# Second mixer: decayed keys and queries built by doubling blocks out of products of f, in place of logarithm, scan and exponentials

## The reference, cut to what matters

```
f = lbf + (1.0 - lbf) * jax.nn.sigmoid(f_logit)      # decay of every key channel and token, between 0 and 1
k = 1.0 - f
logf = jnp.log(f)
...
ac = jnp.cumsum(to_chunks(logf, A_KDIM), axis=3)
def step(S, inp):
    o_inter = jnp.einsum('bhtk,bhkv->bhtv', q_ * jnp.exp(a_), S)
    diff = a_[:, :, :, None, :] - a_[:, :, None, :, :]
    decay = jnp.exp(jnp.where(causal, diff, -jnp.inf))
    scores = jnp.einsum('bhtsk,bhsk->bhts', q_[:, :, :, None, :] * decay, k_)
    o = o_inter + jnp.einsum('bhts,bhsv->bhtv', scores, v_)
    S = jnp.exp(a_last)[..., None] * S + jnp.einsum('bhsk,bhsv->bhkv', k_ * jnp.exp(a_last - a_), v_)
```

## Time and profile before

| what | value |
|---|---|
| median of 3 runs | 2967.06 us (2964.86 to 2969.84) |
| the profiled execution | 2965.61 us, of which the span of its instructions 2963.5 us |
| PE busy | 2866.3 us (97%) |
| DVE busy | 2015.3 us (68%) |
| ACT busy | 1204.7 us (41%) |
| POOL busy | 1214.6 us (41%) |
| slots of `mixer2` in the trace | 1447 to 2037 us |

### The profile page before, as it was taken

How to read it: one execution, slowest core, us unless ns; L and a number is a source line. 1 busy time by engine, 2 the same in 40 slices (tenths; PEclk the granted TensorE clock), 3 DMA queues, 4 the chain that set the end, 5 groups by cost and what they waited for, 6 DMA issues and landing times. The chain is left out here.

```text
span 2963.5 us, 55833 instructions
## 1 busy us (share of the span) xinstructions
PE 2866.3 (97%) x21908; PEld 2485.4 (84%) x21908; DVE 2015.3 (68%) x2754; ACT 1204.7 (41%) x1872; POOL 1214.6 (41%) x1033
## 2 busy tenths in 40 slices
PE   7999999999999999989999999999999999999998
PEld 6787888787888888878989999888978888888886
DVE  6898865568777777677376767674435667666655
ACT  3232544444333333344356565654333333233333
POOL 0002432327565665541344444432223655655552
PEclk9999999999999999999999999999999999999999
DMA  3111000312121111133111111112430211112112
GB/s 127 45 50 36 3 3 25 116 69 59 47 60 46 55 51 53 43 108 107 44 51 51 30 51 30 51 49 87 153 109 29 61 47 54 53 46 60 46 46 85
DMA packets 205491, 173.20 MB, mean 58 GB/s; under 512 B 10589, under 2 KB 182197, under 8 KB 204917
## 3 DMA queue, kind: packets, MB, share of 16 engines
q1 hardware_dynamic: 198389, 161.95, 17.8%
q10 hardware_dynamic: 6912, 8.52, 0.8%
HBM read 149.34 MB, written 21.10 MB: 58 GB/s over the span
## 5 line engine op out<-in xcount | busy, mean ns | idle before, releaser
L3944 PE MATMUL mix_e<-blk_hi,mix_w_hi 128*128 128x348 f32 (+3 forms) x1056 | 350.2, 332 | 1.4 <-DVE blk_lo L3049 1.2
L3094 DVE TENSOR_TENSOR tokens_x<-ffn_acc,tokens_x 128x512 f32<-128x512 f32 x450 | 301.9, 686 | 67.1 <-PE ffn_acc L2650 67.0
L3944 PE MATMUL mix_e<-blk_lo,mix_w_hi 128*128 128x348 f32 (+3 forms) x1056 | 342.9, 325 | 0.0
L3944 PE MATMUL mix_e<-blk_hi,mix_w_lo 128*128 128x348 f32 (+3 forms) x1056 | 341.6, 323 | 0.0
L2633 PE MATMUL ffn_out<-ffn_T,ffn_w12h 128*128 128x512 f32 x1008 | 311.9, 391 | 4.3 <-POOL ffn_w12l L2511 2.2
L2650 PE MATMUL ffn_acc<-blk_hi,ffn_hid_hi 128*128 128x512 f32 x900 | 310.7, 394 | 2.9 <-issue 2.9
L2511 POOL TENSOR_TENSOR ffn_w03l<-ffn_r,ffn_w03h 128x512 fp32r<-128x512 f32 x126 | 193.5, 1536 | 121.4 <-ACT ffn_w03h L2862 117.9
L2633 PEld LDWEIGHTS ffn_out<-ffn_T,ffn_w12h 128*128 128x128 f32 x1008 | 187.7, 188 | 44.1 <-POOL ffn_w12l L2511 2.8
L3464 POOL TENSOR_TENSOR mix_w_lo<-mix_raw,mix_w_hi 128x1024 fp32r<-128x1024 f32 x44 | 107.7, 2448 | 255.2 <-ACT mix_w_hi L3516 255.0
L2511 POOL TENSOR_TENSOR ffn_w12l<-ffn_r,ffn_w12h 128x512 fp32r<-128x512 f32 x114 | 166.7, 1472 | 106.3 <-ACT ffn_w12h L2862 104.4
L3944 PEld LDWEIGHTS mix_e<-blk_hi,mix_w_hi 128*128 128x128 f32 x1056 | 202.0, 191 | 6.1 <-DVE blk_lo L3049 1.4
(11 more groups left out here) (533 smaller groups left out, 7463.0 us busy)
## 6 DMA issues: line engine op xcount, KB each, us to landing
ffn_r<-ffn_up SPq DMA_DIRECT2D x88, 256.0 KB, 3.0
mix_raw<-w_in SPq DMA_DIRECT2D x44, 512.0 KB, 3.8
ffn_r<-w_up SPq DMA_DIRECT2D x88, 256.0 KB, 3.0
ffn_room<-ffn_down SPq DMA_DIRECT2D x20, 512.0 KB, 4.0
ffn_room<-w_down SPq DMA_DIRECT2D x20, 512.0 KB, 4.1
proj_w_raw<-w_in_first SPq DMA_DIRECT2D x19, 512.0 KB, 3.8
branch_gates<-proj SPq DMA_DIRECT2D x16, 520.0 KB, 4.7
wout_raw<-w_out SPq DMA_DIRECT2D x16, 512.0 KB, 4.0
```

The lines of the kernel that those rows point to most:

```text
L3094: return vec.tensor_tensor(dst, accs[t % len(accs)], dst, ALU.add)
L3944: last = nc.tensor.matmul(dst[:, 0:m], a[n % 2][:, kd, :], b[:, kd, c:c + m], start=kd == 0 and part_ == 0, stop=kd == KD - 1 and part_ == 2)
```

## The change

f is no longer turned into logarithms. Keys and queries decayed over blocks of 2^l tokens are turned into those of blocks twice as long by one more factor, the product of f over a neighbouring block of 2^l tokens. POOL makes these block products (`decay_totals`: seven small products for each unit, 128 columns, then 64, 32 and so on to 2). Each doubling (`double(u, l)` on DVE) sees four blocks of 2^l tokens: it writes the two outer ones into the next level's operand `z` (the product called inner factor, L3791 of the new file), and the two inner ones into a second buffer `y` (L3793 of the new file). Since the inner ones are wanted unchanged in the next level's operand as well, ACT copies them from `y` to `z` (`move`, L3605). Level 0 starts with two products of every second token (L3779, L3780) and two copies of every second key by ACT (`move_keys`, L3597, L3598); the last step (`whole_tiles` on DVE, L3805, L3808; `move_ends` on ACT, L3613, L3616) gives the keys to the end of the tile and the queries from its start. The score matmuls read k for level 0 and z for the rest; their number and shapes stay. The floor under f, the scan, both exponentials and the constants of the scan go (one DMA less). TensorE's waits in `scores`, `keys` and `outputs` have one semaphore more.

The diff, cut to POOL's products, ACT's copies, DVE's products and one wait of TensorE:

```diff
+            def decay_totals(u):
+                for l in range(TOTALS):
+                    if l == 0:
+                        pool.wait_ge(f_ready, u + 1)
+                    else:
+                        pool.wait_ge(total_ready, TOTALS * u + l)
+                    whole = total(u, l)[:, 0:2 * total(u, l + 1).shape[1]].rearrange("p (b h) -> p b h", h=2)
+                    tt(total(u, l + 1), whole[:, :, 0], whole[:, :, 1], ALU.mult).then_inc(total_ready, 1)
...
             for u in range(slots):
-                dense = pieces_of_slot(u)
-                for l in range(1, LEVELS2):
-                    if u + 1 < slots:
-                        distances(u + 1, l)
-                    if l == 3:
-                        weight_lo_by(dense[0])
-                    if l == 5:
-                        weight_lo_by(dense[1])
-                for p in dense[2:]:
+                if u + 1 < slots:
+                    decay_totals(u + 1)
+                for p in pieces_of_slot(u):
                     weight_lo_by(p)
...
+            def move_keys(u):
+                act.wait_ge(tree_ready, tree(u, 1))
+                if u:
+                    act.wait_ge(moved, moved_by(u, 0))
...
+                activation(near[:, :, 0], keys_[:, :, 0], ACT.Copy).then_inc(moved, 1)
+                activation(far[:, :, 1], keys_[:, :, 1], ACT.Copy).then_inc(moved, 1)
+
+            def move(u, l):
+                c, n = 2 ** l, level_width(u, l + 1)
+                act.wait_ge(tree_ready, tree(u, BASE + 2 * l))
+                if not l:
+                    act.wait_ge(moved, moved_by(u, 2))
+                activation(quarters(z[u % 2][:, l + 1, 0:n], c)[:, :, 1:3, :], quarters(y[:, 0:n], c)[:, :, 1:3, :],
+                           ACT.Copy).then_inc(moved, 1)
+
+            def move_ends(u):
...
+                act.wait_ge(tree_ready, tree(u, TREE))
                 if u:
                     await_piece(act, "kt", u - 1)
...
+                activation(keys_[:, :, 1, :], far[:, :, 1, :], ACT.Copy).then_inc(moved, 1)
+                if u >= 3:
+                    act.wait_ge(out_ready, number(u - 3, tiles_of(u - 3)[-1]) + 1)
+                activation(queries_[:, :, 0, :], far[:, :, 0, :], ACT.Copy).then_inc(moved, 1)
...
-                vec.tensor_scalar(f, f, LN_FLOOR, None, ALU.max).then_inc(floor_ready, 1)
-                dve.wait_ge(floor_ready, u + 1)
-                vec.tensor_tensor(z[u % 2][:, 0, 0:width(u)], q[:, h % 2, cols_of(u)], f, ALU.mult).then_inc(z_ready, 1)
+                if u:
+                    dve.wait_ge(moved, moved_by(u, 0))
+                vec.tensor_tensor(near2[:, :, 1], q2[:, :, 1], f2[:, :, 1], ALU.mult).then_inc(tree_ready, 1)
+                vec.tensor_tensor(far2[:, :, 0], q2[:, :, 0], f2[:, :, 0], ALU.mult).then_inc(tree_ready, 1)
+
+            def double(u, l):
+                c, n, done = 2 ** l, level_width(u, l + 1), BASE + 2 * l
+                near, wider, far = (quarters(t, c) for t in (z[u % 2][:, l, 0:n], z[u % 2][:, l + 1, 0:n], y[:, 0:n]))
+                sizes = total(u, l)[:, 0:n // c].rearrange("p (b j c) -> p b j c", j=4, c=1)
+                inner, outer = (sizes[:, :, j, :].broadcast_to((P, n // (4 * c), 2, c)) for j in (slice(1, 3), slice(0, 4, 3)))
+                if l:
+                    dve.wait_ge(total_ready, TOTALS * u + l)
+                dve.wait_ge(moved, moved_by(u, l + 2))
+                dve.wait_ge(tree_ready, tree(u, done - 1))
+                vec.tensor_tensor(wider[:, :, 0:4:3, :], near[:, :, 0:4:3, :], inner, ALU.mult).then_inc(tree_ready, 1)
+                dve.wait_ge(moved, moved_by(u, l + 3))
+                vec.tensor_tensor(far[:, :, 1:3, :], near[:, :, 1:3, :], outer, ALU.mult).then_inc(tree_ready, 1)
...
             def scores(u, i):
-                pe.wait_ge(z_ready, PRODUCTS * (u + 1))
+                pe.wait_ge(tree_ready, tree(u, TREE - 1))
+                pe.wait_ge(moved, moved_by(u, LEVELS2 + 1))
```

More of the change, by code:

```diff
@@ L3610, in keys_turned @@
+                activation(queries_[:, :, 0, :], far[:, :, 0, :], ACT.Copy).then_inc(moved, 1)
+                if width(u) > UNIT:
+                    activation(qa[:, u % 3, UNIT:UNIT + 8], y[:, UNIT:UNIT + 8], ACT.Copy).then_inc(moved, 1)
             def keys_turned(u):
@@ L3878, in vector @@
             forget(0)
-            scan(0)
-            queries(0)
-            for l in range(1, LEVELS2):
-                level(0, l)
-            last_keys(0)
+            for l in range(LEVELS2 - 1):
+                double(0, l)
+            whole_tiles(0)
             for u in range(slots):
@@ L3890, in vector @@
                     forget(u + 1)
-                    scan(u + 1)
-                    queries(u + 1)
-                if more:
-                    level(u + 1, 1)
+                    double(u + 1, 0)
                 if spreading:
```

211 lines of the change are left out of this document (92 added, 119 removed).

## The result

The changed kernel takes 2940.11 us (median of 4 runs, 2939.49 to 2941.73) against 2968.45 for the kernel before (4 runs, 2964.86 to 2973.74): a ratio of 0.9904, 95% interval 0.9887 to 0.9921. The profiled executions are 2965.61 before and 2939.49 after, 26.1 us apart; the forecast had 21.3 of that.

The account below looks back on a forecast made before the run. TensorE, busy 97%, was taken as the bound; shorter waits (14.8 us) plus half clock (7.5) less 1 for added semaphores gave 21.3 us, from 2965.6 to 2944.3. Adjusted to the runs' median, the forecast was 2946 us, range 2932 to 2962.

Parts of the forecast that it names:

- What can be won: In the 32 slots: TensorE's 23.4 us idle plus seven units of half clock at 1.5 us, 34 us in all.
- unit of half clock: A 3.41 us stretch of TensorE at 1.2 GHz after a wait, costing 1.5 us; five of seven go, 7.5 us.
- Slots 2 and 27: TensorE's mask waits of 3.41 and 2.84 us there: about 3.0 each stay, gain 0.3.
- Slots 19 and 22: TensorE's mask waits of 2.34 and 3.10 us there: both go, gain 5.4.
- Slot 11: A small mask wait of about 1.0 us following a head, expected to become 1.3.
- State: TensorE's four waits for the state on DVE, 4.0 us, the longest 1.57: all go, gain 4.0.
- The small ones: Eight small mask waits, 5.8 us together: they go except slot 11's, gain 4.5.
- The head 1.6 later, the chain 2.2 shorter, the product less 0.4: Slots 2 and 27: later head activation, shorter ACT way to the piece copy, one DVE product fewer; 1.0 us earlier.
- Here 2.2 of table loads, and the scan, decide.: In slots 19 and 22, 2.2 us of table loads and the scan were said to make the masks late.
- The hold decides, not the loads: Rival: POOL's hold of a DVE product makes masks late; only 12 us gained, 2955 us, chance 0.2.
- All waits go: Rival: slots 2 and 27 lose their waits too; 33 us gained, 2934 us, chance 0.2.
- Slower: Rival: DVE becomes the bound from 0.54 us a product; 2995 us at 0.6, 3048 at 0.72, chance 0.07.

Follow-up runs that it names:

- e2: Changed kernel with a tiny logarithm and exponential, each loading its table, put in every slot on ACT behind the copy of the turned keys; 2942.47 us.
- e3: Changed kernel with a head's activation on ACT put ahead of the unit's sixth move and the end copies; 2936.44 us.
- e4: Changed kernel with the third move ahead of the first dense piece's copy on ACT, and doublings 1 and 2 ahead of the state on DVE; 2933.08 us.
- e10: Changed kernel with only the third move put ahead of the copy of a slot's first piece, DVE's order unaltered; 2937.31 us.
- e7: Kernel before with the slots' logarithm and exponentials made Identity, so no tables load there and other decays are computed; 2951.59 us.
- e6: Kernel before, loads kept, with level 2's exponential ahead of the first piece's copy and its products ahead of the state on DVE; 2956.15 us.
- e9: Kernel before with the edits of e6 and e7 together, computing other decays; 2950.11 us.
- e5: Changed kernel with the edits of e3 and e4 together; 2934.06 us.
- e8: Changed kernel with each of the twelve products of a unit's doublings issued once more on DVE, into a spare tile; 2952.43 us.
- e1: Changed kernel with a tiny logarithm and exponential, each loading its table, put ahead of every unit's key copies on ACT; 2971.52 us.

## Why the prediction was right, point by point

- **What can be won.** Idle time and 1.5 us for each unit of half clock: right; a unit measured 1.3 to 1.7. Five units gone, 7.6 us; forecast 7.5. That it was five is in part luck: in e2 the two waits that I left with their units had none, and that would have been 3 us more.
- **Waits.** Forecast 14.8, measured 15.45. Slots 2 and 27: about 3.0 each stay, measured 2.74 and 2.25. Slots 19 and 22: gone, as said. Slot 11: forecast 1.3, measured 0.85. State: forecast and measured none left (the longest before was 1.64 at 1617, not 1.57). The small ones: gone.
- **The head 1.6 later, the chain 2.2 shorter, the product less 0.4.** Measured 1.2, 2.1, and the mask 1.3 earlier where 1.0 was forecast. That the head behind `move_ends` costs anything is shown by e3, that the hold does by e4 and e10.
- **The step that was wrong** is not in the sum but under it: "Here 2.2 of table loads, and the scan, decide." The 2.2 was right as a difference of two chains. But I put it down to the loads and the scan. e7 shows that of 2.6 us of loads 0.5 (slot 19) to 1.3 (slot 2) came through; under the rest lay ACT's waiting for DVE and POOL. The two slots had 5.44 us of wait, of which the loads alone took 1.90 (e7). For slot 22 the sentence is wrong in a second way: a held product stood ahead of its mask (1866.51, 2.25 us), and with the hold moved and all loads in place its 3.10 fell to 0.25 (e6). Loads, logarithm, scan and their hand-offs left together, so the sum came out.
- **Prices.** Copies: taken 0.35, measured 0.31 (0.22 from start to start). The two key copies, two moves and what lies between: taken 1.7, measured 1.58 (1511.80 to 1513.38). DVE's product: taken 0.29, measured 0.28 to 0.30 when free, but the next starts 0.21 later; the slower rival counted sixteen at 0.29. POOL's seven: 2.0 us in all, in the bounds, though the widest lasts 0.49, over the 0.40 that was the most for each. TensorE's 136 semaphores: taken 1, measured nothing clear (busy without half clock 526.6 to 527.3 with them; before, less 7 units of 1.5, 527.1; idle time of the changed kernel outside the listed waits about 0.5).
- **What the sum lacked.** 26.1 less 21.3 is 4.8: 1.0 for the semaphores, 0.75 in waits and clock, 3.0 behind the stretch, by which unchanged code differed from run to run. The medians are 28.3 apart, because the kernel before's median lay 2.8 above its profiled execution in the second set of runs and the changed one's 0.6.
- **Rivals.** "The hold decides, not the loads": neither alone (e6 takes 10.3 off the stretch, e7 10.4, the change 23.1). In slots 2, 22 and 27 the hold's place decided more than the loads did: e6 took 8.5 of their 9.35 us, e7 3.3. "All waits go", 2934: not by the change, but by one more reordering (e3, e4). "Slower": DVE has room; even 12 more products a slot, 2.2 us, leave the kernel 0.5% faster than before. A product at 0.54, where the rival begins, was not tried.

## What to carry to other kernels

An instruction that leaves a queue is worth its length only if nothing else would have kept the queue waiting there: look for what the engine's next instruction needs, and when that is ready. When a step with many hand-offs between engines is turned into products of one engine, count the hand-offs as well as the instructions: here the loads alone were 10.4 us of the stretch and all the rest 12.6. And look where a hold goes when it is moved: in slot 8 of e9 it fell on the scan, with 2.8 us of wait behind it, in slot 2 of e4 on a product behind the mask, where nobody waited. And after such a change try the order once more: a small copy moved ahead of a weight split took a held product out of the chain and 4.2 us off the stretch (e10), with two doublings (four products) moved on DVE 7.1 us (e4, 2933.08 us, 1.1% less than before, interval 0.9 to 1.3%); e5 stands level with it.

## What the runs showed of the hardware that I had not expected

- Waits of like length don't always bring half clock. The changed kernel's 2.74 and 2.25 were each followed by a unit of 3.41 us at 0.50; in e2 waits of 2.69 and 2.31 in the same places were followed by none. In e8 a wait of 2.01 had none behind it and 2.29 had one; in e9 one of 1.42 had one. I had read from the earlier trace rows that a wait of 1.5 us brings it; it doesn't always.
- DVE's products of 128 columns last 0.28 to 0.30 in the trace and start 0.20 to 0.21 apart, also with runs of one or two elements; ACT's strided copies last 0.31 and start 0.22 apart.
- POOL's products of few columns hardly get cheaper: 0.25 us for 16 columns, against 0.49 for 128.
- A hold isn't confined to the last product of a chain: the first doubling, whose factor is f itself, averages 0.70 us in the changed kernel (24 of 128 columns) where a free one takes 0.30, and in slots 8 and 11 of e7 and e9 the scan is held for 2.65 to 2.69.
- A switch of table costs 1.30 us from the load's start to the activation's in e1 (1514.20 to 1515.50), so two cost 2.9 with their tiny functions. The Trainium skill's page "ScalarE: Activation LUTs", in the section on what a load costs, gives 1.28 for the load, which the rows agree with, and a drain of 1.38 besides, which they don't show here.
